# Spatial gate, head norms and rotation in one stage, q roots in the softmax scale, one weight ring for both halves

## What is computed

```python
def gmlp_group(u, v, v_norm_g, w_s, b_s):
    v = rms_norm(v, v_norm_g).reshape(b, s // CHUNK, CHUNK, GM_GROUPS, GM_GROUP_DIM)
    mixed = jnp.einsum('gij,bnjgc->bnigc', w_s, v) + b_s.T[None, None, :, :, None]
    return u * mixed.reshape(b, s, GM_WIDTH)
...
def gqa_group(q, k, v, q_norm_g, k_norm_g, cos, sin):
...
    q = apply_rope(rms_norm(q, q_norm_g), cos, sin) * (HEAD_DIM ** -0.5)
    k = apply_rope(rms_norm(k, k_norm_g), cos, sin)
...
        sc = jnp.einsum('bkgqd,bskd->bkgqs', qb, k, preferred_element_type=jnp.float32)
        p = jax.nn.softmax(sc, axis=-1).astype(v.dtype)
        return jnp.einsum('bkgqs,bskd->bkgqd', p, v)
```

## Time and profile before

| | |
|---|---|
| median of 3 runs | 3833.82 us (3833.78 to 3835.17) |
| profiled execution | 3838.45 us, span 3837.2 us |
| TensorE (PE) busy | 3427.2 us, 89% |
| VectorE (DVE) busy | 1827.6 us, 48% |
| ScalarE (ACT) busy | 1094.9 us, 29% |
| GpSimd (POOL) busy | 268.7 us, 7% |
| HBM read | 590.17 MB, 154 GB/s over the span |

### The profile page before, as it was taken

How to read it: one execution, slowest core, us unless ns; L and a number is a source line. 1 busy time by engine, 2 the same in 40 slices (tenths; PEclk the granted TensorE clock), 3 DMA queues, 4 the chain that set the end, 5 groups by cost and what they waited for, 6 DMA issues and landing times. The chain is left out here.

```text
span 3837.2 us, 55521 instructions
## 1 busy us (share of the span) xinstructions
PE 3427.2 (89%) x23714; PEld 2398.3 (63%) x23714; DVE 1827.6 (48%) x2870; ACT 1094.9 (29%) x1837; POOL 268.7 (7%) x216
## 2 busy tenths in 40 slices
PE   7789879998878997999979777769999999899999
PEld 6467533332746853333257766656888879678887
DVE  3564433322456443332244555546665462766645
ACT  3353300000335330000032222222433432544333
POOL 1011000000101100000020222200000110010001
PEclk9799989999979998999989888889999999899999
DMA  5022169999402216999932000011222222122322
GB/s 207 12 88 88 55 288 427 427 427 428 174 12 88 88 45 287 427 428 427 427 134 82 3 3 3 2 42 50 88 104 95 88 95 82 45 94 88 110 77 77
DMA packets 49815, 595.84 MB, mean 155 GB/s; under 512 B 5377, under 2 KB 7681, under 8 KB 14081
## 3 DMA queue, kind: packets, MB, share of 16 engines
q1 hardware_dynamic: 49568, 592.29, 38.4%
HBM read 590.17 MB, written 2.10 MB: 154 GB/s over the span
## 5 line engine op out<-in xcount | busy, mean ns | idle before, releaser
L601 PE MATMUL psum<-source_hi,weights_hi 128*128 128x512 f32 (+1 forms) x2352 | 917.6, 390 | 76.6 <-DVE weights_lo L502 68.6
L601 PE MATMUL psum<-source_lo,weights_hi 128*128 128x512 f32 (+1 forms) x2352 | 909.0, 386 | 0.0
L601 PE MATMUL psum<-source_hi,weights_lo 128*128 128x512 f32 (+1 forms) x2352 | 908.9, 386 | 0.0
L601 PEld LDWEIGHTS psum<-source_hi,weights_hi 128*128 128x128 f32 x2352 | 447.2, 190 | 175.6 <-DVE weights_lo L502 81.8
L601 PEld LDWEIGHTS psum<-source_lo,weights_hi 128*128 128x128 f32 x2352 | 447.4, 190 | 89.8 <-issue 2.6
L601 PEld LDWEIGHTS psum<-source_hi,weights_lo 128*128 128x128 f32 x2352 | 447.0, 190 | 88.7
L1405 PE MATMUL psum<-weight_ring_first,branches 128*64 128x512 f32 x2048 | 467.2, 599 | 17.3 <-DMA weight_ring_first<-in_w_up 8.7
L455 ACT CAST weights_hi<-weight_ring_second 128x1024 fp32r<-128x1024 f32 (+3 forms) x230 | 230.7, 1008 | 594.1 <-PE psum L601 575.8
L502 DVE TENSOR_TENSOR weights_lo<-weight_ring_second,weights_hi 128x1024 fp32r<-128x1024 f32 (+3 forms) x230 | 271.9, 1185 | 242.7 <-ACT weights_hi L455 242.0
L1405 PEld LDWEIGHTS psum<-weight_ring_first,branches 128*64 128x64 f32 x2048 | 138.5, 137 | 306.7 <-issue 273.2
L1558 DVE TENSOR_TENSOR x<-psum,x 128x512 f32<-128x512 f32 x256 | 164.3, 685 | 202.4 <-PE psum L1438 202.4
(11 more groups left out here) (362 smaller groups left out, 4319.4 us busy)
## 6 DMA issues: line engine op xcount, KB each, us to landing
weight_ring_first<-in_w_gate SPq DMA_DIRECT2D x64, 2048.0 KB, 17.6
weight_ring_first<-in_w_up SPq DMA_DIRECT2D x64, 2048.0 KB, 18.8
lent_weights<-in_w_down SPq DMA_DIRECT2D x64, 2048.0 KB, 17.7
weight_ring_second<-in_ffn_w_up SPq DMA_DIRECT2D x22, 2048.0 KB, 7.7
weight_ring_first<-in_xattn_w_kv SPq DMA_DIRECT2D x8, 2048.0 KB, 7.7
weight_ring_second<-in_ffn_w_down SPq DMA_DIRECT2D x8, 2048.0 KB, 7.7
weight_ring_first<-in_w_in SPq DMA_DIRECT2D x6, 2048.0 KB, 25.1
weight_ring_second<-in_mix_w_in SPq DMA_DIRECT2D x6, 2048.0 KB, 8.4
```

Source lines behind the costliest of these rows:

```text
L601: ins = pe.matmul(ps, a, b, start=k == 0 and q == 0, stop=k == job.rows // P - 1 and q == 2)
```

## The change

1. `spatial_gate`, `head_norms` and `rope` become one stage, `gate_and_heads`. Its SP part loads the rotation tables, then the gate's weights and bias. All head squares are on VectorE. ScalarE multiplies the tiles of q and k by the norm's gain before the rotation, and VectorE rotates the tiles without their roots. The gate's gain and bias are one pass. Only the k tile is multiplied by its spread roots, after the rotation. `head_norms` stays in use in the second half.
2. The roots of q, times the scale and its negative, lie in a small tile `q_roots` of [128, 2, 4, 4, 2]. `paired_attention` reads from it the scale of the exponential and the factor of the maximum.
3. One `Ring` holds the pieces of both halves. It has 2 slots for the whole run, 2 more while the first half lasts, and the 2 lent ones of the experts. The two slots can be loaded for the second half as soon as the pieces of the first half are issued.

```diff
-RING, RING_2, LENT = 4, 2, 2
+RING, RING_1, LENT = 2, 2, 2
...
-    def __init__(self, nc, ctx, whole, pieces, name, slots, lent=0):
-        tile = ctx.enter_context(nc.sbuf_tensor(f"weight_ring_{name}", [P, slots, KT * SLOT_COLS], F32))
-        self.landed = [whole.enter_context(nc.semaphore(f"weights_landed_{name}{i}")) for i in range(slots + lent)]
-        self.used = whole.enter_context(nc.semaphore(f"weights_used_{name}"))
+    def __init__(self, nc, ctx, pieces, slots, lent):
+        tile = ctx.enter_context(nc.sbuf_tensor("weight_ring", [P, slots, KT * SLOT_COLS], F32))
+        self.landed = [ctx.enter_context(nc.semaphore(f"weights_landed{i}")) for i in range(slots + lent)]
+        self.used = ctx.enter_context(nc.semaphore("weights_used"))
         self.pieces, self.own = pieces, slots
...
-    def lend(self, tiles, until):
-
-        for i, tile in enumerate(tiles):
-            self.tiles[self.own + i], self.last[self.own + i], self.until[self.own + i] = tile, -1, until
+    def lend(self, tiles, until, at=0):
+
+        for i, tile in enumerate(tiles, self.own + at):
+            self.tiles[i], self.last[i], self.until[i] = tile, -1, until
...
-                dve.tensor_scalar(st[:, b, NMAX], st[:, b, MAX], -scale, None, ALU.mult).then_inc(nmax_ready, 1)
+                p, qt = divmod(j, TT)
+                dve.tensor_tensor(st[:, b, NMAX], st[:, b, MAX], roots[:, 1, p, qt, :], ALU.mult).then_inc(nmax_ready, 1)
...
-                    act.activation(prob[:, b, a, :], src, ACT.Exp, bias=st[:, b, 2 + a:3 + a], scale=scale,
+                    act.activation(prob[:, b, a, :], src, ACT.Exp, bias=st[:, b, 2 + a:3 + a],
+                                   scale=roots[:, 0, j // TT, j % TT, a:a + 1],
...
-def rope(K, qk, tiles):
...
-def spatial_gate(K, l, u, v, cols, values, vv):
+def gate_and_heads(K, l, u, v, values, vv, qk, q_root, gate_gain, q_gain, k_gain, scale):
...
+        SUMS, MIX, SWAP = 7, 3, 0
 
         @block.sync
         def _(sp):
-            sp.dma_start(ws[:, :, :], K.dram["gm_w_s"][l].rearrange("j (g i) -> j g i", g=4)).then_inc(landed, 16)
+            sp.dma_start(tab[:, :, :], K.dram["rope"].rearrange("(a p) t -> p a t", p=P)).then_inc(rope_landed, 16)
+            sp.dma_start(ws[:, :, :], K.dram["gm_w_s"][l].rearrange("j (g i) -> j g i", g=4)).then_inc(gate_landed, 16)
             src = K.dram["gm_b_s"][l:l + 1, :].to_broadcast([P, 512])
-            sp.dma_start(bs[:, :, :], src.rearrange("p (g i) -> p g i", g=4)).then_inc(landed, 16)
+            sp.dma_start(bs[:, :, :], src.rearrange("p (g i) -> p g i", g=4)).then_inc(gate_landed, 16)
...
-            act.activation(st[:, 1, :], st[:, 0, :], ACT.Sqrt, bias=K.eps[:, 0:1], scale=1.0 / 512)\
-                .then_inc(root, 1)
+            act.activation(st[:, 1, :], st[:, 0, :], ACT.Sqrt, bias=K.eps[:, 0:1], scale=1.0 / 512).then_inc(v_root, 1)
+            for i in range(5):
+                act.wait_ge(squared, i + 1)
+                act.activation(qk[:, i, :], qk[:, i, :], ACT.Copy, scale=q_gain if i < 4 else k_gain).then_inc(scaled, 1)
+            act.wait_ge(summed, 5)
+            act.activation(roots[:, :, :, :].rearrange("p i t h -> p (i t h)"), K.psum[:, SUMS, 0:10 * TT], ACT.Sqrt,
+                           bias=K.eps[:, 0:1], scale=1.0 / HEAD).then_inc(root, 1)
             act.wait_ge(turned, 1)
-            link(act.copy(vv[:, :, :], K.psum[:, 4, :].rearrange("p (t f) -> p t f", f=P)))
+            link(act.copy(vv[:, :, :], K.psum[:, MIX + 3, :].rearrange("p (t f) -> p t f", f=P)))
 
         @block.tensor
         def _(pe):
             for t in range(TT):
-                ins = pe.transpose(K.psum[:, 4, t * P:(t + 1) * P], values[:, t * P:(t + 1) * P], K.ident)
+                ins = pe.transpose(K.psum[:, MIX + 3, t * P:(t + 1) * P], values[:, t * P:(t + 1) * P], K.ident)
             ins.then_inc(turned, 1)
-            pe.wait_ge(landed, 32)
-            pe.wait_ge(normed, TT)
-            for g in range(4):
+            for i in range(5):
+                pe.wait_ge(squared, i + 1)
+                sum_heads(pe, K, K.psum[:, SUMS, 2 * TT * i:2 * TT * (i + 1)], squares[:, i % 3, :]).then_inc(summed, 1)
+
+            def swap(i):
+                pe.wait_ge(scaled, i + 1)
+                if i >= 3:
+                    pe.wait_ge(swap_kept, i - 2)
+                pe.matmul(K.psum[:, SWAP + i % 3, :], K.swap, qk[:, i, :], start=True, stop=True).then_inc(swapped, 1)
+
+            def blend(g):
                 for n in range(TT):
-                    ins = pe.matmul(K.psum[:, g, n * P:(n + 1) * P], v[:, n, g * P:(g + 1) * P], ws[:, g, :],
+                    ins = pe.matmul(K.psum[:, MIX + g, n * P:(n + 1) * P], v[:, n, g * P:(g + 1) * P], ws[:, g, :],
                                     start=True, stop=True)
                 ins.then_inc(mixed, 1)
+
+            swap(0)
+            swap(1)
+            pe.wait_ge(gate_landed, 32)
+            pe.wait_ge(v_normed, TT)
+            blend(0)
+            blend(1)
+            swap(2)
+            blend(2)
+            pe.wait_ge(alink, TT + 1)
+            blend(3)
+            swap(3)
+            swap(4)
+            pe.wait_ge(inverse, 1)
+            spread_heads(pe, K, K.psum[:, SUMS, :], roots[:, 4]).then_inc(spread, 1)
 
         @block.vector
         def _(dve):
             link = linker(dve, dlink)
-            dve.wait_ge(root, 1)
+            for i in range(5):
+                if i >= 3:
+                    dve.wait_ge(summed, i - 2)
+                dve.tensor_tensor(squares[:, i % 3, :], qk[:, i, :], qk[:, i, :], ALU.mult).then_inc(squared, 1)
+            dve.wait_ge(v_root, 1)
             link(dve.reciprocal(st[:, 2, :], st[:, 1, :]))
             for t in range(TT):
-                dve.tensor_scalar(v[:, t, :], v[:, t, :], st[:, 2, t:t + 1], None, ALU.mult).then_inc(normed, 1)
-            dve.wait_ge(landed, 32)
-            for g in range(4):
+                dve.tensor_scalar(v[:, t, :], v[:, t, :], st[:, 2, t:t + 1], None, ALU.mult).then_inc(v_normed, 1)
+
+            def rotate(i):
+                dve.wait_ge(scaled, i + 1)
+                link(dve.tensor_tensor(part[:, 0, :], qk[:, i, :], tab[:, 0, :], ALU.mult))
+                dve.wait_ge(swapped, i + 1)
+                dve.tensor_tensor(part[:, 1, :], K.psum[:, SWAP + i % 3, :], tab[:, 1, :], ALU.mult).then_inc(swap_kept, 1)
+                dve.wait_ge(swap_kept, i + 1)
+                link(dve.tensor_tensor(qk[:, i, :], part[:, 0, :], part[:, 1, :], ALU.add))
+
+            def gate(g):
                 dve.wait_ge(mixed, g + 1)
-                link(dve.tensor_scalar(mix[:, :], K.psum[:, g, :], cols[:, g:g + 1], None, ALU.mult))
-                link(dve.tensor_tensor(mix[:, :].rearrange("p (n i) -> p n i", n=TT),
-                                       mix[:, :].rearrange("p (n i) -> p n i", n=TT),
-                                       bs[:, g:g + 1, :].to_broadcast([P, TT, P]), ALU.add))
+                link(dve.scalar_tensor_tensor(out=mix[:, :].rearrange("p (n i) -> p n i", n=TT),
+                                              in0=K.psum[:, MIX + g, :].rearrange("p (n i) -> p n i", n=TT),
+                                              scalar=gate_gain[:, g:g + 1], in1=bs[:, g:g + 1, :].to_broadcast([P, TT, P]),
+                                              op0=ALU.mult, op1=ALU.add))
                 link(dve.tensor_tensor(u[:, g, :], u[:, g, :], mix[:, :], ALU.mult))
+
+            dve.wait_ge(rope_landed, 16)
+            rotate(0)
+            rotate(1)
+            dve.wait_ge(root, 1)
+            dve.reciprocal(roots[:, :, :, :], roots[:, :, :, :]).then_inc(inverse, 1)
+            dve.wait_ge(inverse, 1)
+            dve.wait_ge(gate_landed, 32)
+            gate(0)
+            gate(1)
+            rotate(2)
+            gate(2)
+            gate(3)
+            rotate(3)
+            rotate(4)
+            dve.tensor_scalar(q_root[:, 0], roots[:, 0:4], scale, None, ALU.mult)
+            dve.tensor_scalar(q_root[:, 1], roots[:, 0:4], -scale, None, ALU.mult)
+            dve.wait_ge(spread, 1)
+            dve.tensor_tensor(qk[:, 4, :], qk[:, 4, :], K.psum[:, SUMS, :], ALU.mult)
...
+            q_root = K.sbuf(inner, "q_roots", [P, 2, 4, TT, 2])
...
-                spatial_gate(K, l, u, v, c("gm_v_norm_g", 4), values, vv)
-            head_norms(K, [([qk[:, t, :] for t in range(4)], c("q_norm_g", 1)), ([qk[:, 4, :]], c("k_norm_g", 1))])
-            rope(K, qk, range(5))
...
-                             out_of=lambda p: att[:, p, :], scale=HEAD ** -0.5)
+                             out_of=lambda p: att[:, p, :], roots=q_root)
...
-            ring.lend(lent, ring.fed + 6 * NE)
+            ring.lend(lent, ring.fed + 6 * NE, RING_1)
...
+        K.ring = Ring(nc, ctx, first_pieces + second_pieces, RING, RING_1 + LENT)
         with ExitStack() as first:
-            K.ring = Ring(nc, first, ctx, first_pieces, "first", RING, LENT)
```

(35 more changed lines are left out.)

11 lines of the change are left out of this document (9 added, 2 removed).

## The result

The changed kernel takes 3776.72 us (median of 4 runs, 3771.68 to 3777.8) against 3834.49 for the kernel before (4 runs, 3833.78 to 3839.19); the ratio is 0.9842, 95% interval 0.9828 to 0.9857. The forecast was 3773.5 with 3764.5 to 3787.0. Its profiled execution took 3775.7, 62.75 less than the profiled one of before (3838.45); the sum forecast 60.3. TensorE's share of the span went from 89% to 90%, VectorE's stays at 48%.

A forecast was written before the change was run, and what follows sets the result against it. TensorE was taken as busy most of the span, but not the bound in the gate-to-rotation stretch, at the experts' DMA and at the seam. Stages 47.1 plus seam 13.2 gave 60.3 off 3833.8, so 3773.5 us, range 3764.5 to 3787.

The forecast's parts named there:

- The seam: Between the two halves: ScalarE's whole wait for the second half's first weights goes, 13.2 us.
- The stage: Merged gate, head norms and rotation: ends at 131.8 in place of 155.37, gaining 23.6 us a layer.
- Step (d): First swap queued behind all five sums, in at 114.1; VectorE gets 2.3 us of new wait; rotation tables arrive in time.
- (b): TensorE's five head sums from 105.2, two at full clock and three at half, done at 112.2.
- Step (e): After the first swap VectorE is the bound; its passes sum to 17.7 us, ending the stage at 131.8.
- the cover: TensorE's blends, swaps and spread come before VectorE asks, even at half clock; thinnest margin some 0.7 us, at the blends.
- the price of the exponential: In attention: a column as scale leaves the exponential near 0.70 us, judged by a silu at 0.69.
- the 0.75 that was to show the step wrong: Sign against the forecast, in attention: an exponential taking over 0.75 us.
- The small product: In attention, for the negated maximum: tensor_tensor in place of tensor_scalar, 0.15 to 0.35 us, costing 0 to 5, taken as 0.
- The first: Rival, merged stage: clock stays at 2.4 GHz through sums and swaps, gain 25.9 a layer, 3768.8 us; chance 0.16.
- The second: Rival: attention starts at the higher clock, at most 2 us a layer more, 3769.5 us; chance 0.11.
- The third and fourth: Rivals: the seam yields nothing, 3786.7 us, chance 0.08; the column scale slows attention's exponential, 3837.5 us, chance 0.03.

The follow-up runs named there:

- two_rings: Changed kernel with the two separate weight rings of before, one for each half; 3790.07 us, ratio 0.9877 to the kernel before.
- early_swaps: Changed kernel with two swaps ahead of the last two head sums, squares in five buffers, reciprocal after the gate; 3771.24 us, run again 3769.35.
- early_pool: early_swaps with the gate's last product with u moved from VectorE to GpSimd, into four buffers; 3770.47 us.
- before_tables: Kernel before with one edit, the rotation tables loaded in the gate's stage; 3831.24 us against 3838.16.
- before_merged: Kernel before with one edit, the gate's gain and bias in one VectorE pass; 3831.64 us against 3838.16.
- constant_scale: Changed kernel with 1/8 as a constant in first-half attention's exponential and negated maximum, q roots unused; 3775.79 us.
- after_again: Changed kernel unaltered, run once more as base of the second group; 3776.92 us against 3838.16 for the kernel before.
- all_spread: Changed kernel with the roots of all five tiles spread and multiplied in by VectorE, and a constant scale in attention; 3778.05 us.

## Why the prediction was right

**The seam** was forecast at 13.2 and measured at 13.3 by the marks and 13.0 by the wait that came back in two_rings, with the loads issued at the moment forecast (the used gate piece). The early loads cost the last expert at most 0.9 us, and not in every execution.

**The stage** was forecast to gain 23.6 in each layer; it gained 23.0 and 23.9. Step (d) named the wait that takes the place of the removed ones, for the first swap behind five sums. It has 3.47 and 2.54 where 2.3 was given. The term that was mis-sized is (b): the sums were taken with a clock that falls 2.5 us after the stage's start. In layer 0 it fell 1.8 after it (105.7 − 103.9), and the sums took 7.78 in place of 6.96. In layer 1 it fell 2.8 after the start, the sums took 6.85, and the first swap was in 9.62 after the start, as forecast (114.1 − 104.5 = 9.6). Step (e), VectorE as the bound with 17.7, came out as 17.51, and the cover held: no wait at the blends. early_swaps shows the wait to be on the path, since taking it out shortens the stage by all of it; early_pool shows VectorE to be the bound of the rest, since the stage follows its passes. before_tables (3.4 a layer) and before_merged (3.1) price two of the parts; together with the roots in the scale (at most 2) they are not half of the 23. The rest is, by difference, the merging: the squares, sums, swaps and roots that now fill waits, and two changes of stage. No run takes that part alone.

**Attention.** The step that failed is the price of the exponential: put at 0.70 by the silu with a column as scale, it is 0.81, above the 0.75 that was to show the step wrong. The silu has one column; this exponential has two, scale and bias, and that of before had one already. The Trainium skill ("ScalarE: Activation LUTs", What ACT_TABLE_LOAD costs) says that each column operand adds some 93 ns. The medians of constant_scale and the changed kernel differ by 106 ns and the minima by 89, so the trace agrees. The error cost little, 0.7 us a layer, because in most steps ScalarE has a wait that takes in the longer exponential. The small product took 0.16 like the pass that it replaces.

**The rivals.** The first (clock stays up through the sums) did not come: the clock was down from the second sum on in layer 0, from the third in layer 1. The second came in one layer of two, and by luck. Its condition was that TensorE ends its work some three microseconds ahead of attention. TensorE ended 9.13 and 8.18 ahead, since the blends and the spread ran at the higher clock, and attention began at the lower clock in both layers. That the clock then rose after 4 us in layer 0 is not the edit's doing: the same stage in two_rings was followed by 9 low microseconds. In layer 0 the first copy came 7.49 after attention's start in place of 9.14, and the last step ran at the higher clock (2.27 in place of 3.15), together 2.5 us; the exponential took some of that back, and 1.75 were left. In layer 1 the start was no faster, and the last step gained only what the exponential cost. The third and fourth did not come.

**The sum** of 60.3 compares with 62.75 between the profiled executions, with 57.8 between the medians of the first group and with 61.2 between those of after_again's. The stages and the seam alone, which are the terms of the sum, gained 23.0 + 23.9 + 13.3 = 60.2. The changed kernel's two medians agree within 0.2 us; those of the base lie 3.7 apart. The first median lies 3.2 above the forecast, which is within that scatter.

## What to carry to other kernels

When stages in a row leave their engines waiting in turns, lay the new order out engine by engine from measured durations, and look for the instruction that stands in a queue behind work which its reader does not need; here that was worth 2.2 to 3.1 us a layer. A ring that ends with one part of a program and begins anew in the next makes the next part wait for its first load, here 13.2 us. An operand moved from a constant to a column has a price that depends on how many columns the instruction has already: compare with a row that has as many.

## What the runs showed of the hardware that was not expected

- A second column operand made an exponential of 128x512 with accumulation 106 ns longer (700 to 806).
- TensorE's granted clock fell from 1.00 to 0.50 while it worked without a gap on head sums of two columns each, and stayed down for 10 us, through the rest of the sums and two swaps.
- The same instructions of attention, with the constant scale, took 60.69 and 63.71 us in one execution (all_spread): the clock rose 3.0 us into them or 8.5, and was low near their end for 3 to 4 us or for 6 to 7.
- The same unchanged second half took 1883.24 us in one execution and 1886.98 in another.
- VectorE's product of two SBUF operands took up to 1.79 in place of 0.69 beside a GpSimd product of the same size.
